# Layer 0's modulation vector: shift on TensorE, scale and gate on VectorE, the gate a stage later

## The reference

```python
silu_c, silu_cc = jax.nn.silu(c), jax.nn.silu(c_ctx)
for l in range(DEPTH):
    mod_x = silu_c @ w_ada[l] + b_ada[l]      # (1, 3072)
    mod_c = silu_cc @ w_ada[l] + b_ada[l]
    shift, scale, gate = split(mod, 3)
    h = rmsnorm(x, g_pre) * (1 + scale) + shift
    p = h @ w_in[l]                           # projections of four branches
    y = merge(attention, conv, retention, fourier, ...) @ w_out[l]
    x = x + gate * rmsnorm(y, g_post)
```

## Time and profile before

| | us |
|---|---|
| median of 3 runs | 2599.12 |
| lowest, highest | 2592.25, 2603.63 |
| the profiled execution: its own time | 2598.11 |
| its span | 2596.1 |
| TensorE busy | 2490.1 (96%) |
| VectorE, ScalarE, GpSimd busy | 1141.2, 1114.5, 1221.2 |
| mean TensorE clock granted | 0.991 of full |

### The profile page before, as it was taken

How to read it: one execution, slowest core, us unless ns; L and a number is a source line. 1 busy time by engine, 2 the same in 40 slices (tenths; PEclk the granted TensorE clock), 3 DMA queues, 4 the chain that set the end, 5 groups by cost and what they waited for, 6 DMA issues and landing times.

```text
span 2596.1 us, 38839 instructions
## 1 busy us (share of the span) xinstructions
PE 2490.1 (96%) x12993; PEld 2086.3 (80%) x12993; DVE 1141.2 (44%) x1698; ACT 1114.5 (43%) x2329; POOL 1221.2 (47%) x996
## 2 busy tenths in 40 slices
PE   7888999999999999999999989999999999999998
PEld 1887987898888777787888778898888788888887
DVE  2453657394345432333343456691535423333322
ACT  2646564496212454434433443793214333343333
POOL 1567983122222378855555442122213455555554
PEclk9899999999999999999999999999999999999999
DMA  6346761100120255544433431001211333344333
GB/s 251 90 137 179 215 196 61 33 1 22 51 63 27 61 159 158 161 118 148 131 107 106 162 102 49 9 1 42 65 37 33 104 109 109 113 136 145 109 109 133
DMA packets 393274, 262.38 MB, mean 101 GB/s; under 512 B 16935, under 2 KB 365751, under 8 KB 391611
## 3 DMA queue, kind: packets, MB, share of 16 engines
q1 hardware_dynamic: 378944, 227.07, 29.8%
q10 hardware_dynamic: 14204, 33.67, 3.7%
HBM read 251.23 MB, written 9.45 MB: 100 GB/s over the span
## 4 chain that ended last, share of the span: by engine, by line
PE 82%; POOL 6%; issue 4%; DVE 4%; ACT 2%; DMA 1%; DVEq 0%; ACTq 0%; POOLq 0%; SPq 0%
PE ps L744 78%; POOL w_lo L640 4%; PE ps L936 2%; POOL w_lo L633 2%; DMA w_raw<-in_w_in 1%; DVE r_prev L2156 1%; DVE softmax_stats L2049 1%; PE ps L776 0%; DVE a_probT_lo L1792 0%; DMA w_ada<-in_w_ada 0%; DVE a_out_sum L1792 0%; PE ps L876 0%; ACT w_hi L1279 0%; PE ps L922 0%; ACT a_prob L1450 0%
## 5 line engine op out<-in xcount | busy, mean ns | idle before, releaser
L633 POOL TENSOR_TENSOR w_lo<-w_raw,w_hi 128x512 fp32r<-128x512 f32 x644 | 877.1, 1370 | 976.6 <-ACT w_hi L1279 970.7
L744 PE MATMUL ps<-hT_hi,w_hi 128*128 128x512 f32 (+1 forms) x2528 | 944.1, 373 | 42.1 <-POOL w_lo L640 17.0
L744 PE MATMUL ps<-hT_lo,w_hi 128*128 128x512 f32 (+1 forms) x2528 | 930.9, 368 | 0.0
L744 PE MATMUL ps<-hT_hi,w_lo 128*128 128x512 f32 (+1 forms) x2528 | 930.7, 368 | 0.0
L1279 ACT ACTIVATE w_hi<-w_raw 128x512 fp32r<-128x512 f32 x760 | 472.0, 629 | 927.0 <-PE ps L744 839.9
L744 PEld LDWEIGHTS ps<-hT_hi,w_hi 128*128 128x128 f32 x2528 | 480.2, 190 | 136.6 <-issue 14.2
L744 PEld LDWEIGHTS ps<-hT_hi,w_lo 128*128 128x128 f32 x2528 | 480.5, 190 | 78.8
L744 PEld LDWEIGHTS ps<-hT_lo,w_hi 128*128 128x128 f32 x2528 | 480.9, 190 | 75.1
L1792 DVE TENSOR_TENSOR merge_tmp<-merge_tmp,ps 128x512 f32<-128x512 f32 (+1 forms) x160 | 101.5, 634 | 660.0 <-PE ps L744 409.1
L640 POOL TENSOR_TENSOR w_lo<-w_raw,w_hi 128x512 fp32r<-128x512 f32 x116 | 155.5, 1365 | 42.3 <-ACT w_hi L1279 42.0
L1792 DVE TENSOR_TENSOR merge_tmp<-merge_tmp 128x512 f32<-128x512 f32 (+1 forms) x120 | 165.9, 1382 | 4.1
(11 more groups left out here) (272 smaller groups left out, 3001.0 us busy)
## 6 DMA issues: line engine op xcount, KB each, us to landing
w_raw<-in_w_in SPq DMA_DIRECT2D x476, 256.0 KB, 2.9
w_raw<-in_w_o_rest SPq DMA_DIRECT2D x112, 256.0 KB, 2.8
w_raw<-in_w_out SPq DMA_DIRECT2D x74, 256.0 KB, 2.6
w_ada<-in_w_ada SPq DMA_DIRECT2D x8, 1536.0 KB, 9.6
w_raw<-in_w_ada SPq DMA_DIRECT2D x48, 256.0 KB, 2.7
w_raw_more<-in_w_in SPq DMA_DIRECT2D x72, 128.0 KB, 2.5
w_raw<-in_w_o_attn SPq DMA_DIRECT2D x32, 256.0 KB, 2.8
w_raw<-in_dft_x SPq DMA_DIRECT2D x16, 256.0 KB, 2.7
```

The source lines that it names most:

```text
L633: eng.tensor_tensor(w_lo[:, r, :], raw[:, r, :], w_hi[:, r, :].bitcast(F32), ALU.subtract).then_inc(sem["w_split"], tally.up("w_split"))
L744: return eng.matmul(dst, lhsT, rhs, start=start, stop=stop)
```

## The change

Only layer 0's modulation vector is made in another way.

- **Loads.** Each slice of w_ada is loaded without its gate third: shift and scale, 1 MB in two DMAs. The gate's 4 MB follow in four DMAs behind slices 6 and 7.
- **Shift** stays on TensorE: 2 matmuls a slice, 16 in all; 8 transposes.
- **Scale** goes to VectorE. For every slice k and stream s it adds w[k] (128 x 1024) times the scalar column silu_cT[s, k] to an accumulator in SBUF (n_tmp): 16 instructions of 1024 elements, the first two a tensor_scalar, the others a scalar_tensor_tensor. The tokens' `scaled` runs between k = 3 and k = 4. The 128 partial sums of a column are then added by TensorE: 16 fp32 matmuls with the accumulator as stationary operand (128 x 128) and one column of ones moving, straight into column layout. VectorE adds bias and one, and multiplies with norm_pre.
- **Gate** goes to VectorE too, one stage pair later: 16 such instructions (`gate_sums`) after attention, ahead of the context's convolution. Behind the R tiles TensorE adds the partitions (`gate_columns`, 16 matmuls of one column), VectorE adds the bias and multiplies with norm_post (`gate_from_columns`), TensorE turns the result (`turn_gate`), ScalarE saves it and issues its DMA (`save_gate`). TensorE waits for the save before it ends the stage.

The diff, without the lines that only set up names:

```diff
@@ SP: modulation
-                for k in range(KT):
-                    ada(p.layer, k)
+                for k in range(KT):
+                    if k > 1:
+                        eng.wait_ge(ada_in[k - 2], 32)
+                    for half in range(2):
+                        eng.dma_start(ada_part(k, half), w[k * P:(k + 1) * P, half * D:(half + 1) * D].rearrange(
+                            "p (a n) -> p a n", a=2)).then_inc(ada_in[k], 16)
+                for k in range(0, KT, 4):
+                    eng.wait_ge(ada_in[KT - 2 + k // 4], 32)
+                    for half in range(2):
+                        eng.dma_start(w_ada_head[:, half, k:k + 4, 0:512], w[k * P:(k + 4) * P, 2 * D + half * 512:2 * D + (half + 1) * 512]
+                                      .rearrange("(k p) n -> p k n", p=P)).then_inc(sem["gate_w_in"], 16)
@@ PE: modulation
-                    for n in range(6):
-                        ins = mm(ps[0:2, n, :], sT[:, :, k], w_ada[:, k, n * 512:(n + 1) * 512], k == 0, k == KT - 1)
+                    for n in range(2):
+                        ins = mm(ps[0:2, n, :], sT[:, :, k], ada_part(k, n // 2)[:, n % 2, :], k == 0, k == KT - 1)
...
-                eng.wait_ge(sem["mod_saved"], tally.take("mod_saved", 6))
-                for c in range(2 * KT):
+                eng.wait_ge(sem["scale_sum"], tally.take("scale_sum", 2))
+                for s in range(2):
+                    for c in range(KT):
+                        last = mm(ps[:, 7, s * KT + c:s * KT + c + 1], n_tmp[:, 2 * s + c // 4, c % 4 * P:(c % 4 + 1) * P], small[:, 0:1], True, True)
+                last.then_inc(sem["scale_added"], tally.up("scale_added"))
+                eng.wait_ge(sem["mod_saved"], tally.take("mod_saved", 2))
+                for c in range(KT):
@@ PE: R tiles of the first pass
                 project(p, 6)
+                if p.opens:
+                    gate_columns()
...
                 turn_values(p, R_V + 1, R_V)
+                if p.opens:
+                    turn_gate(1)
+                    eng.wait_ge(sem["gate_saved"], tally.take("gate_saved"))
                 stage_end(eng, tally, "pe")
@@ ACT
-                eng.wait_ge(sem["gate_made"], tally.take("gate_made"))
-                eng.dma_start(gate_rows[l], m_gate[0:2, :]).then_inc(sem["gate_out"], tally.up("gate_out", 16))
-                eng.wait_ge(sem["gate_out"], tally.now("gate_out"))
...
                 tile_range(p, R_Q, R_Z)
+                if p.opens:
+                    save_gate(p.layer, 1)
                 stage_end(eng, tally, "act")
@@ DVE: modulation
-                scaled(p, 0)
-                for n in range(6):
+                for k in range(KT):
+                    if k == 4:
+                        scaled(p, 0)
+                    eng.wait_ge(ada_in[k], 32)
+                    for s in range(2):
+                        acc, w = n_tmp[:, 2 * s:2 * s + 2, :], ada_part(k, 1)
+                        if k == 0:
+                            ins = eng.tensor_scalar(acc, w, sT[:, s, 0:1], None, ALU.mult)
+                        else:
+                            eng.wait_ge(sem["dve_own"], tally.now("dve_own", s - 1 if k == KT - 1 else -1))
+                            ins = eng.scalar_tensor_tensor(acc, w, sT[:, s, k:k + 1], acc, ALU.mult, ALU.add)
...
+                for n in range(2):
@@ DVE: stages B and R of the first pass
                 attention(p)
                 stage_end(eng, tally, "dve")
+                if p.opens:
+                    gate_sums()
                 convolution(p)
                 decay_tables()
...
                 r_keys(p)
+                if p.opens:
+                    gate_from_columns()
                 stage_end(eng, tally, "dve")
```

More of the change, by code:

```diff
@@ L974, in attention, with gate_columns, turn_gate @@
                         turn(g - 1, 1)
+            def gate_columns():
+                eng.wait_ge(sem["gate_sum"], tally.take("gate_sum", 2))
+                for s in range(2):
+                    for c in range(KT):
+                        last = mm(ps[:, 1, 256 + s * KT + c:257 + s * KT + c], gate_acc(s)[:, c // 4, c // 2 % 2, c % 2 * P:(c % 2 + 1) * P],
+                                  small[:, 0:1], True, True)
+                last.then_inc(sem["gate_added"], tally.up("gate_added"))
+            def turn_gate(bank):
+                eng.wait_ge(sem["gate_cols"], tally.take("gate_cols"))
+                eng.transpose(ps[0:2 * KT, bank, 0:P], n_gate[:, :, :], ident[:, :]).then_inc(
+                    sem["gate_turned"], tally.up("gate_turned"))
             def late_keys(after, p):
@@ L1664, in merge @@
                 if ada:
-                    eng.wait_ge(sem["gate_turned"], tally.take("gate_turned"))
-                    act(n_gate_row[0:2 * KT, :], ps[0:2 * KT, 0, 0:P]).then_inc(sem["gate_saved"], tally.up("gate_saved"))
-                    eng.wait_ge(sem["gate_saved"], tally.now("gate_saved"))
-                    eng.dma_start(gate_rows[p.layer + 1].rearrange("s (c p) -> (s c) p", p=P), n_gate_row[0:2 * KT, :]).then_inc(
-                        sem["gate_out"], tally.up("gate_out", 16))
+                    save_gate(p.layer + 1, 0)
                 split_high(1)
@@ L1847, in next_modulation @@
                 eng.wait_ge(sem["dve_own"], tally.now("dve_own"))
[L1848 to L1850 removed]
+                gate_products()
                 for s in range(2):
@@ L1875, in modulation, with gate_sums @@
                 for s in range(2):
                     eng.tensor_copy(mod[:, s, 1, :], cols[:, 0:KT, s]).then_inc(sem["dve_own"], tally.up("dve_own"))
-                    eng.scalar_tensor_tensor(mod[:, s, 0, :], cols[:, KT:2 * KT, s], 1.0, gpre[:, :],
-                                                  ALU.add, ALU.mult).then_inc(sem["dve_own"], tally.up("dve_own"))
                 eng.wait_ge(sem["dve_own"], tally.now("dve_own"))
+            def gate_sums():
+                eng.wait_ge(sem["gate_w_in"], tally.take("gate_w_in", 64))
+                for k in range(KT):
+                    for s in range(2):
+                        if k == 0:
+                            ins = eng.tensor_scalar(gate_acc(s), gate_part(0), sT[:, s, 0:1], None, ALU.mult)
+                        else:
+                            eng.wait_ge(sem["dve_own"], tally.now("dve_own", s - 1 if k == KT - 1 else -1))
+                            ins = eng.scalar_tensor_tensor(gate_acc(s), gate_part(k), sT[:, s, k:k + 1], gate_acc(s), ALU.mult, ALU.add)
+                        name = "gate_sum" if k == KT - 1 else "dve_own"
+                        ins.then_inc(sem[name], tally.up(name))
@@ new lines, in gate_from_columns @@
+            def gate_from_columns():
+                eng.wait_ge(sem["small_in"], tally.take("small_in", 32))
+                eng.wait_ge(sem["gate_added"], tally.take("gate_added"))
+                for s in range(2):
+                    tt(n_sum[:, s, 2 * KT:3 * KT], ps[:, 1, 256 + s * KT:256 + (s + 1) * KT], n_bias[:, 2 * KT:3 * KT], ALU.add).then_inc(
+                        sem["dve_own"], tally.up("dve_own"))
+                eng.wait_ge(sem["dve_own"], tally.now("dve_own"))
+                gate_products()
@@ L1881, in mean, with gate_products @@
+            def gate_products():
+                for s in range(2):
+                    ins = tt(n_gate[:, s, :], n_sum[:, s, 2 * KT:3 * KT], n_post[:, :])
+                    ins.then_inc(sem["gate_cols"], tally.up("gate_cols")) if s else ins.then_inc(sem["dve_own"], tally.up("dve_own"))
             def mean(p, b):
```

65 lines of the change are left out of this document (40 added, 25 removed).

## The result

| | us |
|---|---|
| changed kernel: median of 5 runs (lowest, highest) | 2613.51 (2612.59, 2619.05) |
| kernel before on the same chip: median of 5 | 2598.8 (2592.25, 2603.63) |
| ratio, 95% interval | 1.0064, 1.0047 to 1.0081 |
| the profiled execution: own time, span | 2612.59, 2610.6 |
| forecast | 2610, range 2597 to 2618 |

The change makes the kernel 14.7 us slower by the medians. Its time lies inside the range, 3.5 over the predicted one. It is just past the 13 us that I had set as the border, so it falls into "slower" (0.38) and not "within 0.5%" (0.57). Both ends of the interval are slower; its lower end is on the other side of the border.

A forecast was written before the change was run, and what follows sets the result against it. TensorE, holding 82% of the chain, was taken as the bound. Start -7.0, B stage +13 and R stage +5.5 sum to +11.5 on 2598.1, giving 2609.6, or 2610.6 on the median; stated as 2610, range 2597 to 2618.

The forecast's parts named there:

- B: Context's B stage: gate_sums on VectorE alternates with GpSimd's w_lo and delays the stage's end; +13 us, bounds +2 and +18.
- A: Start: fewer TensorE matmuls and transposes, path now VectorE's, first norm_tmp at 50.8 instead of 58.06; -7.0 us, bounds -12 and 0.
- C: Context's R stage: gate_columns on TensorE plus the chain behind r_v make all wait; +5.5 us, bounds +2 and +9.
- I let log_gamma end about 2 us sooner: Start: with fewer bytes ahead of the small tables, log_gamma ends at 22 instead of 23.8.
- over 12: Start: TensorE idle over 12 us before the scale's one-column matmuls, likened to the stretch before 99; records taken as 6.0 us.
- The rival on the tokens: Start: token DMAs still queue behind w_ada and the gate's 4 MB, arriving at 37.9; sum +19, 2617 us; chance 0.16.
- lands after about 32: Start: deciding point for the late-tokens case, the second token tile landing after about 32 us.
- tokens that land past 32: Start: one of the prediction's stated signs of being wrong; its own estimate had the second token tile near 29.3 us.
- B costs little: B stage rival: GpSimd is starved, so few instructions pair; +3 us there, sum +1.5, 2600 us; chance 0.18.
- the dearer pair: B stage rival: a VectorE and GpSimd pair takes 2.58 us, adding 5 us, 2615 us in all; chance 0.08.
- TensorE's own time: 32 x 0.11: R stage: gate_columns' 32 records between the last R tile and the fill cost 3.5 us, bounds 1.0 and 7.0.
- Layer 1 and everything behind 200 us ... shift as a whole: After the first 200 us: work is unchanged and only shifts as a whole, with the same bytes.

The follow-up runs named there:

- the kernel of 3: The change with the gate's accumulators in PSUM, only the last instruction of each writing to SBUF; 2604.66 us, ratio 1.0021 to the kernel before.
- 1: The change with gate_sums cut to its two k = 0 instructions and gate_columns to one matmul; 2598.86 us, ratio 1.0004 to the kernel before.
- 2: The change with gate_sums cut to its two k = 0 instructions and gate_columns whole; 2599.47 us, ratio 1.0005 to the kernel before.
- 6: The change with gate_columns moved ahead of the R tiles and turn_gate behind them; 2604.09 us, ratio 1.0026 to the kernel before.
- 7: The change with eight extra 512-column matmuls on TensorE ahead of the scale's partition sums; 2611.86 us, ratio 1.0052 to the kernel before.
- Experiment 4: The change with token tiles requested before the small-table wait and log_gamma's steps woven between VectorE's slices; 2606.86 us, ratio 1.0040 to the kernel before.
- 8: The change with gate accumulators in PSUM, the reordered start and gate_columns ahead of the R tiles; 2586.35 us, repeated 2587.41; ratios 0.9952 and 0.9950.
- 9: The kernel of 8 with five extra 512-column matmuls on TensorE ahead of the scale's partition sums; 2589.17 us, ratio 0.9959 to the kernel before.

## Why the forecast was nearly right

The main mechanism was right in all three parts, and B to a tenth. A and C were mis-sized, both on the favourable side: 3.9 and 2.5, which makes the sum 17.8 instead of 11.5. The ratio measured twice, 1.0064, is 16.6. That the first median is only 3.5 from the forecast is in part luck: in the change's first trace the terms are 6.3 off together, and the work behind 200 us gave 3.3 of it back.

**Part A, forecast -7.0, measured -3.1: mis-sized.** VectorE was through at 46.3 and not at 43.4. "I let log_gamma end about 2 us sooner", because fewer bytes lay ahead of the tables, failed: in the trace it ends where it ended. The runs show that no single number stood for it, and why stays open: with the same start the tables came at 18.2 (the change, twice, and the kernel of 3) or at 14 to 15.2 (1, 2, 6, 7). As ScalarE issues the tokens behind log_gamma, they carry the tables' delay too, and the second tile, used 9.2 after its issue at 23.23, took 1.1 more than the forecast had for it (its 8.5 counted from the first tile's issue, its 14.6 for the kernel before from the second's; by the second's it is 8.1). It is used at 32.42, not 29.3, and VectorE ends 2.9 late. The one-column records at half clock took 6.99 and not 6.0: 1.0. The half clock had been forecast from a poor likeness: TensorE had waited 8.3 and not "over 12", and ahead of 99, in the kernel before, it was idle for some 3. And token transposes at half clock behind the modT columns held the first norm_tmp back by 0.35 more. That is the 4.2 between 50.8 and 55.01. The slices were not in by 31 either, the last one came at about 35.3, but VectorE was later still. The rival on the tokens named "lands after about 32" as its point, and "tokens that land past 32" was among the prediction's own signs of being wrong; the landing was 32.4. So by its own sign A was wrong in this wait, though the price, +0.5 to +1 for A, was far too high, because it assumed 37.9. Experiment 4 shows what the two waits were worth, 6.8 at the partition sums. Here VectorE's path was the right one and its size too generous, within the bounds of -12 and 0.

Not settled: what the start alone is worth at the end. With early tables the kernel of 1 turned r_kT 4.9 sooner than before, the chain behind r_v included, but its median is level with before; the interval of 4 us on either side leaves room for a few us and for nothing.

**Part B, forecast +13, measured +12.9: right, step by step.** 2.23 per pair taken from the earlier trace rows, 2.22 measured; the B tiles' last matmuls end at 153.3, which is 156.4 once the 3.1 that the start had gained are put back, as forecast; a tail of 9.5 from b_cu to the R tiles' weights, 164.29 - 154.79 = 9.5. Experiment 3 takes the pairing away and 11.9 of the 12.9 with it; experiment 2 puts gate_sums at 12.3 inside the stretch, and at 14.0 by medians that hold the earlier tables too. The rival "B costs little" and the dearer pair are out.

**Part C, forecast +5.5, measured +8.0 (7.3 in the change's second trace): mis-sized.** The chain at 2.2 (less 0.2) was 2.8. The columns at 32 x 0.11 = 3.5 were 3.9 in experiment 2 and by the same subtraction 5.2 in the change, 4.77 of it the records. The failing step is "TensorE's own time: 32 x 0.11", which took them at full clock; they brought the half clock with them, which I had only in the bound. Moving the part in 6 returned 9.3 in the trace and 10.8 in the median (with an earlier start), so all of C's cost lay in its place.

**"Layer 1 and everything behind 200 us ... shift as a whole"** held in sum and not in a single execution. The three terms measured add to +17.8 at r_kT, and the change's profiled execution ended +14.5. The windows of before show a granted clock of 0.79 over 496 to 504, 858 to 866 and 2002 to 2010, those of the change 1.00 over the same work, some 17 us later. In its second trace the change was 17.0 behind at r_kT and 18.1 at the end. So I take the 3.3 for chance of one execution; that the change has no part in where such stretches fall wasn't tested.

## What to carry to other kernels

Before work is put on an idle VectorE, look at what GpSimd does at that moment: here the same instruction cost 2.22 beside it with its accumulator in SBUF and 1.20 with it in PSUM. Work that only feeds something much later belongs into a stretch in which its engine waits anyway: the same 16 matmuls and the chain behind them cost 8 at the end of a stage and nothing ahead of it. And matmuls of one column are cheap by their count only: in every trace here the clock was at its lower level in them or shortly behind, and the work behind them paid unless it had slack.

## What was not expected of the hardware

- The small tables came at one of two times. The same kernel (8) had them by 15.6 in one execution and at 19.4 in the other, which was on another chip; kernels with the change's own start had them at 14 to 15.2 or at 18.2, on one chip, and never between.
- TensorE counted as busy without a gap and yet lost its clock. In the six traces with gate_columns behind the R tiles (the change twice, and the kernels of 2, 3, 4, 7) the windows show 0.50 to 0.59 right behind 32 fp32 records of one column, after R tiles at full clock; the lower level is 0.50 (1.2 GHz). In 1 and 6, which don't have them there, and in the kernel before it stayed at 1.00 in that place, and in 6 it fell to 0.50 where the records had gone. In the start, matmuls of 512 columns right ahead of such records held it at 0.99 through them once (7) and at 0.88 in the other (9).
- Beside each other the 14 VectorE instructions and GpSimd's w_lo kept the same pitch, 2.22 and 2.23 (four in 8.94), less than the sum of what they take alone (1.28 and 1.30). By the Trainium skill ("SBUF — State Buffer", section "Who interferes with whom") the shared port pair is an exclusive lock, held for the whole instruction; an estimate by that is 1.28 + 1.30 = 2.58. The trace stays under it, and the measurement decides.
